# Turned dilated values, earlier diagonals, two single last tiles and another final norm in a two-block transformer kernel

## What is computed

```python
for l in range(2):
    x = x + 0.5 * swiglu(rmsnorm(x, norm_ffn1[l]), w_ffn1_in[l], w_ffn1_out[l])
    h = rmsnorm(x, norm_mix[l])
    x = x + mixing_sublayer(h, ...)          # retention: each head is normed by itself
    x = x + 0.5 * swiglu(rmsnorm(x, norm_ffn2[l]), w_ffn2_in[l], w_ffn2_out[l])
x = rmsnorm(x, norm_final)                   # end of the first block

mem_n = _rmsnorm(mem, g_mem)                 # second block
h = _rmsnorm(x, g_mix)
proj = h @ w_in                              # q, k, v of three dilated groups are in here
for g, (window, dil) in enumerate(((128, 1), (512, 4), (2048, 16))):
    o_g, lse_g = _dilated_group(q_g, k_g, v_g, table_g, dil, window // dil)
x = x + merged @ w_out
x = x + square(relu(_rmsnorm(x, g_mlp) @ w_mlp_in)) @ w_mlp_out
return _rmsnorm(x, g_final)
```

## Time and profile before

| | us |
|---|---|
| median of 3 runs | 3264.24 (3261.61 to 3267.8) |
| the profiled execution | 3263.25 |
| its span in the profile | 3261.5 |
| TensorE busy in the span | 3203.7 (98%) |
| VectorE, ScalarE, GpSimd busy | 1531.7, 1105.8, 254.6 |
| mean granted TensorE clock | 0.994 of full |

### The profile page before, as it was taken

One profiled execution on the slowest core, in us unless ns is written; L12 is line 12 of the kernel. 1 busy time (PEld: TensorE's weight loads), 2 busy tenths in 40 slices (PEclk: granted clock), 3 DMA queues, 4 the chain that ended last, 5 costly groups with the idle time before them and its releaser, 6 DMA issues.

```text
span 3261.5 us, 37207 instructions
## 1 busy us (share of the span) xinstructions
PE 3203.7 (98%) x15004; PEld 2623.9 (80%) x15004; DVE 1531.7 (47%) x2428; ACT 1105.8 (34%) x1566; POOL 254.6 (8%) x229
## 2 busy tenths in 40 slices
PE   8999999999999999999999999999999999999997
PEld 6888887778888888888877788888888877788886
DVE  5434445555433454344454555334555233454352
ACT  4323335333322332233353333223456233332221
POOL 1000113002000000001120110001100000110001
PEclk9999999999999999999999999999999999999998
DMA  4222321213422232223222233222322232232221
GB/s 133 96 97 94 128 84 65 72 65 97 136 97 97 91 102 96 98 93 112 84 67 69 79 103 98 97 97 90 111 83 81 70 105 84 91 95 99 95 98 67
DMA packets 91551, 303.09 MB, mean 93 GB/s; under 512 B 10228, under 2 KB 16500, under 8 KB 90832
## 3 DMA queue, kind: packets, MB, share of 16 engines
q1 hardware_dynamic: 91380, 300.71, 28.1%
HBM read 298.52 MB, written 5.29 MB: 93 GB/s over the span
## 4 chain that ended last, share of the span: by engine, by line
PE 94%; DVE 2%; issue 2%; ACT 1%; POOL 0%; DMA 0%; SPq 0%; POOLq 0%; DVEq 0%; ACTq 0%
PE bank L1455 87%; PE score_ps L1374 1%; PE score_ps L1309 1%; PE out_ps L1387 1%; PE turn_ps L1278 1%; PE out_ps L1342 1%; PE turn_ps L1320 1%; DVE tmp L1953 0%; PE score_ps L1351 0%; PE turn_ps L1257 0%; PE turn_ps L1329 0%; PE out_ps L1361 0%; ACT w_hi L1483 0%; PE score_ps L1418 0%; DVE tmp L2081 0%
## 5 line engine op out<-in xcount | busy, mean ns | idle before, releaser
L1840 DVE TENSOR_TENSOR w_lo<-raw,w_hi 128x1024 fp32r<-128x1024 f32 (+1 forms) x548 | 677.3, 1237 | 1286.9 <-ACT w_hi L1483 1285.9
L1455 PE MATMUL bank<-in_hi,w_hi 128*128 128x512 f32 x2672 | 1068.7, 400 | 18.5 <-DVE in_lo L1846 11.2
L1455 PE MATMUL bank<-in_hi,w_lo 128*128 128x512 f32 x2672 | 1043.7, 391 | 0.0
L1455 PE MATMUL bank<-in_lo,w_hi 128*128 128x512 f32 x2672 | 1042.7, 390 | 0.0
L1483 ACT ACTIVATE w_hi<-raw 128x1024 fp32r<-128x1024 f32 (+1 forms) x548 | 568.0, 1037 | 1149.6 <-PE bank L1455 1145.1
L1455 PEld LDWEIGHTS bank<-in_hi,w_hi 128*128 128x128 f32 x2672 | 503.5, 188 | 142.9 <-issue 28.4
L1455 PEld LDWEIGHTS bank<-in_hi,w_lo 128*128 128x128 f32 x2672 | 502.8, 188 | 107.6
L1455 PEld LDWEIGHTS bank<-in_lo,w_hi 128*128 128x128 f32 x2672 | 503.7, 189 | 101.1 <-issue 2.4
L1455 PE MATMUL bank<-hid_hi,w_hi 128*128 128x512 f32 x960 | 373.4, 389 | 0.0
L1455 PE MATMUL bank<-hid_lo,w_hi 128*128 128x512 f32 x960 | 373.4, 389 | 0.0
L1455 PE MATMUL bank<-hid_hi,w_lo 128*128 128x512 f32 x960 | 373.4, 389 | 0.0
(11 more groups left out here) (306 smaller groups left out, 2848.5 us busy)
## 6 DMA issues: line engine op xcount, KB each, us to landing
raw<-w_ffn_in SPq DMA_DIRECT2D x176, 512.0 KB, 3.4
raw<-w_mix SPq DMA_DIRECT2D x90, 512.0 KB, 3.4
raw<-w_ffn_out SPq DMA_DIRECT2D x80, 512.0 KB, 3.4
raw<-w_mixb SPq DMA_DIRECT2D x58, 512.0 KB, 3.5
raw<-w_mlp_in SPq DMA_DIRECT2D x32, 512.0 KB, 3.4
raw<-w_mlp_out SPq DMA_DIRECT2D x32, 512.0 KB, 3.4
raw<-w_w_out SPq DMA_DIRECT2D x16, 512.0 KB, 3.4
raw<-w_ffn_out SPq DMA_DIRECT2D x16, 256.0 KB, 2.7
```

The costliest lines, as they stand in the source:

```text
L1455: mm = pe.matmul(ps, lhs, rhs, start=first and step == 0, stop=last and step == 2, skip_group_check=True)
L1840: dve.tensor_tensor(w_lo[:, i % SPLIT, 0:cols], raw[:, i % RAW, 0:cols], w_hi[:, i % SPLIT, 0:cols].bitcast(F32), ALU.subtract).then_inc(S ...
```

## The change

- `dv` of groups 1 and 2: computed features by tokens like queries and keys (48 matmuls of 512 columns each instead of 96 of 256), evicted by VectorE into `tmp` sorted by residue (`evict_dv_turned`), and turned one and two units later by four transposes a tile (`dv_turn`), which ScalarE copies into `dv`.
- `diag` is a step of its own, ahead of `spread`: in the hook of `stats`, in the retention slot where `ret_finish` stood, and with `final_product`. `ret_finish` moves one slot back and to the front of its slot; the final spreads move one unit back.
- `root` takes three Newton steps instead of four. `final_stats` and `final_product` lose the sums by residue.
- `mlp_out`: its last two output tiles are single groups of 8 contraction slices a unit.
- The ending: the last tile's squares go to TensorE without GpSimd's addition; `last_spread` writes the row sums' result twice, into `turn_ps` and `score[0]`; VectorE multiplies six tiles straight out of PSUM; GpSimd multiplies tiles 2 and 5, which ScalarE has already scaled, by the copy in SBUF.

```diff
+LAST_ON_POOL = (2, 5)
+NEWTON = 3
+def but_last(n):
+    return pairs(0, n - 2) + [[n - 2], [n - 1]]
...
     def norm_hooks(self, which="ssum", cols="rcol", dst="rstd", n=TT):
-        self.hooks.extend([lambda: None, lambda: self.stats(which, cols, n), lambda: self.spread(cols, dst, n)])
+        self.hooks.extend([lambda: None, lambda: (self.stats(which, cols, n), self.diag(cols, n)),
+                           lambda: self.spread(cols, dst, n)])
...
-        for n in range(RH * TT + 3):
+        for n in range(RH * TT + 4):
             def ret_slot(n=n):
+                if 0 <= n - 4 < RH * TT and (n - 4) % TT == TT - 1:
+                    self.ret_finish(l, (n - 4) // TT)
                 if n < RH * TT:
                     self.ret_scores(n)
...
                 if 0 <= n - 3 < RH * TT and (n - 3) % TT == TT - 1:
-                    self.ret_finish(l, (n - 3) // TT)
+                    self.diag("hcol", TT, True)
...
+            def evict_dv_turned(outs, units, pair):
+                it = self.item("evict_dv_turned", units=units, pair=pair, rstd=self.vals["rstd", "rstd"], parts=[])
+                for f, o in outs:
+                    part = dict(f=f, o=o, t=self.tmp.take(), v=self.add("dve_evict"))
+                    it["parts"].append(part)
+                    self.after(1 + f, lambda part=part: self.dv_turn(g, part))
+                self.bank_over[pair] = ("dve_evict", part["v"])
+            if g == 0:
+                self.gemm("mixb", DT, [[0, 1]], inp, evict_dv, rows="tok", tok=TT)
+            else:
+                self.gemm("mixb", DT, [[0, 1]], inp, evict_dv_turned)
...
-        self.hooks.extend([lambda: None, lambda: None, self.final_stats, self.final_product,
+        self.hooks.extend([lambda: None, lambda: None, self.final_stats,
+                           lambda: (self.final_product(), self.diag("rcol", TT), self.diag("hcol", TT)), lambda: None,
                            lambda: (self.spread("rcol", "rstd", TT), self.spread("hcol", "final_rstd", TT))])
...
+        for j in LAST_ON_POOL:
+            self.item("last_gain", j=j, out=self.add("x_gained"))
+        self.last_stats()
+        sp = self.last_spread()
...
+            def dv_turn(it):
+                pe.wait_ge(S_["dve_evict"], it["v"])
+                if it["turn"].over:
+                    pe.wait_ge(S_[it["turn"].over[0]], it["turn"].over[1])
+                for r_ in range(DIL):
+                    mm = pe.transpose(tok(r_, turn_ps), tok(r_, tmp[it["t"].b]), ident[:])
+                mm.then_inc(S_["turned"], 1)
...
+                elif kind == "dv_turn":
+                    act.wait_ge(S_["turned"], it["mm"])
+                    act.activation(dv[:, :, it["g"], it["f"] * P:(it["f"] + 1) * P],
+                                   turn_ps.rearrange("p (r c) -> p r c", r=DIL), ACT.Copy).then_inc(S_["act_evict"], 1)
...
+                elif kind == "evict_dv_turned":
+                    dve.wait_ge(S_["rstd"], it["rstd"])
+                    dve.wait_ge(S_["unit_used"], it["units"])
+                    for part in it["parts"]:
+                        if part["t"].over:
+                            dve.wait_ge(S_[part["t"].over[0]], part["t"].over[1])
+                        dst = tmp[part["t"].b].rearrange("p (r j) -> p r j", r=DIL)
+                        dve.tensor_tensor(dst, by_residue(product(it, part["o"])), by_residue(RSTD["rstd"]),
+                                          ALU.mult).then_inc(S_["dve_evict"], 1)
```

More of the change, by code:

```diff
@@ L389, in then_square @@
             self.ssum_place = self.ssum.take()
-        part["square"] = self.square_sum(j, "ssum", self.ssum_place.over if j == 0 else None)
+        if j < DT - 1:
+            part["square"] = self.square_sum(j, "ssum", self.ssum_place.over if j == 0 else None)
+        else:
+            part["square"] = self.last_square = dict(which=None, sq=self.add("square"), place=self.tmp.take())
     def softmax(self, it):
@@ L730, in dil_turn, with dv_turn @@
         self.vals["dil_pt", n] = it
+    def dv_turn(self, g, part):
+        it = self.item("dv_turn", g=g, f=part["f"], t=part["t"], v=part["v"], turn=self.turn.take(), mm=self.add("turned"),
+                       copied=self.add("act_evict"))
+        part["t"].over_at("turned", it["mm"])
+        it["turn"].over_at("act_evict", it["copied"])
+        for r in range(DIL if part["f"] else 0):
+            self.vals["dv", r, g] = it["copied"]
     def dil_values(self, n):
@@ L1852, in low, with root @@
                                   ALU.subtract).then_inc(S_[name + "_lo"], 1)
-            def root(v, n, over, dst, first, last):
+            def root(v, n, over, dst, first, last, more=None):
                 c = [stat_sb[:, i, 0:n] for i in range(8)]
@@ L1860, in root @@
                 dve.wait_ge(S_["stat_in"], first)
+                if more is not None:
+                    step(dve.scalar_tensor_tensor(c[6], more, 1.0 / over, c[0], ALU.mult, ALU.add))
+                    dve.wait_ge(S_["dve_step"], steps[0])
+                    c[0] = c[6]
                 step(dve.tensor_scalar(c[1].bitcast(I32), c[0].bitcast(I32), 1, None, ALU.logical_shift_right))
```

132 lines of the change are left out of this document (97 added, 35 removed).

## The result

| | before | changed |
|---|---|---|
| median, us | 3262.93 (4 runs, 3261.61 to 3267.8) | 3213.1 (4 runs, 3212.1 to 3214.99) |
| ratio | 1 | 0.9845, 95% interval 0.9828 to 0.9862 |
| the profiled execution, us | 3263.25 | 3213.65 |
| its span, us | 3261.5 | 3211.9 |
| mean granted TensorE clock | 0.994 | 0.997 |

What follows compares the result with a forecast made beforehand. PE, busy for 98% of the span, was taken as the bound. Terms of -20.5, -13.5, -2.5, -8.0 and -2.7 summed to -47.2 us against the profiled 3263.25, giving 3216 us, range 3208 to 3227.

Steps and rivals of the forecast that it cites:

- dilated values: Projections: 192 strided matmuls replaced by 96 of 512 columns plus four turns; net -20.5 us, bounds -24 and -17.
- retention, waits and clock: Retention in both layers: PE's waits for diagonals go, -13.5 us, and most half-clock time comes back, -2.5 us.
- end of the first block: Stage of 31.0 us there: shorter sums, no diagonal wait, earlier spreads; -8.0 us, bounds -10 and -5.
- ending: After the last large matmul: 18.2 us instead of 20.9; -2.7 us, bounds -1.5 and -6.
- (a): End of the first block: 16 sum records left of 32, ending at 2307.5 instead of 2310.43; -2.9 us.
- (b): End of the first block: diagonals ready at 2315.5, PE at the spreads at 2316.2, so the 2.63 us wait goes.
- (c): End of the first block: spreads and 48 matmuls done at 2325, before 2335; half clock 3 us at either place.
- What would show it: Signs across the kernel: few diagonal waits outside the ending, stage under 24 us, half clock under 10 us before the ending.
- Waits return one step later: Retention: `ret_finish` delays VectorE's score weighting, 0.7 us at six slots; with other costs 3224.5; chance 0.2.
- The clock stays full: First block's end, ending and memory branch's gates: all low-clock stretches go, giving 3209; chance 0.12.
- The diagonals' buffer: Ring `tmp`: diagonals hold buffers longer, VectorE stalls at some 18 spreads; 3270 at 3 us each; chance 0.03.
- Strided reads of PSUM: New evictions reading every fourth PSUM value slow the matmuls beside them, costing 4 us, 3220; chance 0.03.

Runs made afterwards that it cites:

- e2: Kernel before the change, with weights of `dv` groups 1 and 2 cut from tokens in order instead of every fourth; 3239.72 us.
- e3: Kernel before the change, with weights of `dv` groups 1 and 2 cut as every second token; 3241.06 us.
- e9: Kernel before the change, with weights of `dv` groups 1 and 2 cut as every third token; 3253.5 us.
- e1: Changed kernel, with `dv` of groups 1 and 2 computed tokens by features again, weights cut by residue; 3235.52 us.
- e5: Changed kernel with four Newton steps instead of three; 3216.87 us.
- e6: Changed kernel with the sums by residue made again at the end of the first block and not used; 3218.54 us.
- e10: Changed kernel with the two final spreads and their diagonals in one hook, one unit earlier, as before the change; 3217.03 us.
- e8: Changed kernel with one spread in the ending and VectorE multiplying all eight tiles, GpSimd's two tiles gone; 3212.28 us.
- e12: The changed kernel timed once more, unedited; median 3213.52 us over 4 runs.
- e7: Changed kernel with the last product by pairs of output tiles to its end; 3219.57 us.
- e4: Changed kernel with `ret_finish` put back into the slot of the diagonals, three Newton steps kept; 3225.89 us.

## Why the prediction was right

| term | forecast | measured | from |
|---|---|---|---|
| dilated values | -20.5 | -20.5 | -23.0, and +2.5 for three turns in the attention stage |
| retention, waits and clock | -16.0 | -17.2 | -12.2 and -5.1 |
| end of the first block | -8.0 | -7.2 | 39.53 to 32.30 |
| ending | -2.7 | -3.1 | 21.4 to 18.3 |
| low clock in the attention | 0 | -1.6 | one stretch of 3.4 us less |
| sum | -47.2 | -49.6 | 3261.5 to 3211.9 |

- **Dilated values.** That the strided weight load sets a matmul's distance is shown by e2, e3 and e9, where nothing but the step changed. The +2.5 is the stage's +0.9 with the low stretch that went out of it (1.6) put back, and e1 has it too. The turns came at 2.5 for three, 1.26 of it the wait, so 0.4 for each turn; the forecast had 0.45 each and 1.0 for the wait. The wait's size was near and its cause differed: ScalarE's split stood ahead of the copy, not the copy's own length alone. One bound was added up wrongly: 45.3 less 22.0 is 23.3, and turns at 0.35 us each make it -21.9, not -24. The measured value lies inside either bound.
- **Retention.** All of the 13.5 us of waits went (the trace after), and the finish one slot later took nearly all of it (e5). In layer 1, without low stretches before or after, the 5.1 us are the 4.9 of waits, 0.5 less for the new wait below, and 0.7 more. In layer 0 the large matmul that starts at 683.82 before stands at 679.41, ahead of any low stretch: 4.4 us for two waits of 1.96. So a wait gave back some 0.2 us more than its idle time, in both layers; why is not settled. For the 12.2 of layer 0 there are then 8.6 of waits, 0.8 of this surplus over four waits and, for two low stretches at the 1.6 of the last section, 3.1, together 0.3 more than measured. The forecast had 2.5 for the clock (bound 2.9) and nothing for the surplus; between them these make the 1.2 us by which the term was short.
- **The end of the first block.** The three steps (shorter sums, no wait, spreads a unit earlier) happened as they were written down, and each has its run: e6, e10. The sum by residue was worth 1.7 us, and not the 2.9 that (a) took for it. In (b) the diagonals had 2.3 us to spare where 0.7 was forecast. One low stretch of 6.8 us remained at the sums and none behind the spreads, where (c) counted on 3 us at either of two places. Runs of the same instructions have this stage at 32.3 us with 6.8 us at half clock (e8, e12) or at 30.8 with 3.4 (e7), and the kernel before and its variants e2, e3 and e9 have it at 37.9 to 39.5; so that the term came out within 0.8 us is in part luck.
- **The ending.** GpSimd's first multiplication began 11.1 us after the last large matmul and the third store's tile was written at about 12.35, as the prediction said (11 and 12.3). That six stores would queue behind it is what e8 shows: 1.6 us lost, with the second spread and its copy in the same edit.
- **What would show it** came out: diagonals waited for only in the ending (the forecast's 20 us before hold the ending's 4.1; outside it they were 16.1); one wait of 0.52 us for weighted scores (L2291), in layer 1, just over the 0.5 of the sign; 23.79 us for the stage; 6.8 us of half clock ahead of the ending, under 10.
- **Rivals.** *Waits return one step later* did not: the one wait of 0.5 us is all of it. *The clock stays full* came true in one place: the attention has a low stretch in the profiled run before and none in the one after, which I had put at its price (1.7) but not into the sum. Most of the 2.4 us between forecast and the profiled execution is this. It is luck and not the change: runs before the change have one or two there, runs after it none or two. *The diagonals' buffer*: no wait of the kind is in the trace. *Strided reads of PSUM*: the matmuls beside a new eviction keep their distance, here 0.22 us (changed kernel, timeline):

```profile
2525.34 2.03 DVE L2225 TENSOR_TENSOR tmp<-bank,rstd_b 128x512 f32<-128x512 f32 x2 [3.12 <-PE bank L1554]
...
2525.76 0.39 PE L1554 MATMUL bank<-in_lo,w_hi 128*128 128x512 f32 x1
2525.98 0.40 PE L1554 MATMUL bank<-in_hi,w_lo 128*128 128x512 f32 x1
```

The rule of the Trainium skill that was weighed there ("SBUF — State Buffer", the note on cachelines) doesn't show itself for VectorE's reads of PSUM in this case.

The misses partly cancel: retention gave 1.2 us more than forecast and the end of the first block 0.8 less. What stays open is the clock. Where it falls to half isn't fixed by the program alone: below.

## What to carry to other kernels

Look at the weight load's duration before the matmul's: a float32 operand cut with a step of three or more as weights set the distance of matmuls of 256 columns here, and taking the tokens in order and turning the result cost less; cut two apart it was free. Where PE waits for something that VectorE writes from a result of the same step, move the consumer one slot on before shortening the chain: here that took 12.9 us of waits and a root one step shorter 3.5 at most. At a kernel's end, ask of each helper engine whether it starts later than the engine that it relieves would finish.

## What the runs showed of the hardware

- **A weight load of 128 x 128 float32 values** took 192, 195, 263 and 333 ns with steps of 1, 2, 3 and 4 values.
- **The half clock moves between runs of the same instructions.** Up to the projections e2 and e3 run the same instructions as the kernel before. Their low stretches in layer 0's retention lie at 670.4 and 690.9 us in e2 and at 651.1, 692.1 and 709.1 in e3, against 689.9 and 706.9 before; retention's output comes at 714.10, 715.70 and 713.92. A third stretch is 1.6 us more. In the attention, where e4 to e8, e10 and e12 run the changed kernel's own instructions, it and e4, e8, e10 and e12 had none (273.1 to 273.3 us), e5 to e7 two (276.2 to 276.3). In every such pair a stretch of 3.4 us costs 1.6 us. So the total of one run can't tell an edit's 3 us from this; its stages can. Layer 0's retention and the spreads at the end of the first block differ from that: there low stretches came in every run in which PE waited for diagonals by 2.0 to 2.7 us at the longest, and in none of the others. The two of e5_four_newton in the attention (same columns as the stretches above):

```profile
2673.70:2677.10 3.40, 3.40 (x11) 2.65 (x10) 0.00 (x0) 0.38 (x1) 0.00 (x0) 0.50 0.14 57
2701.00:2704.40 3.40, 3.40 (x10) 2.63 (x10) 0.00 (x0) 0.88 (x2) 0.00 (x0) 0.50 0.34 133
```

PE was busy all through both; ahead of the one at 2673.70 it had stood idle 2.0 us for `tmp` (L2070), a wait that is also in the runs without a low stretch there.
